# Expert results added onto residual rows in DRAM by the scatter, and a tail worked in halves

## The reference, cut to what matters

```python
x = x + mix
x = x + _hier_moe(_rmsnorm(x, norm_ffn_g), ...)      # 16 experts, each token goes to 2 of one group
y = _rmsnorm(x, norm_final_g)                        # rows of 1024; meta rows are dropped

# in _hier_moe, per token and expert:
act = silu(t @ w_gate_e) * (t @ w_up_e) * comb       # comb is 0 for experts not chosen
out = sum over experts of act @ w_down_e
```

## Time and profile before

| | us |
|---|---|
| median of 3 runs | 772.13 (771.56 to 772.36) |
| the profiled execution, device time | 773.97 |
| its span in the trace | 772.1 |
| PE busy | 751.5 |
| DVE busy | 667.1 |
| ACT busy | 515.4 |
| POOL busy | 97.3 |

### The profile page before, as it was taken

One profiled execution on the slowest core, in us unless ns is written; L12 is line 12 of the kernel. 1 busy time (PEld: TensorE's weight loads), 2 busy tenths in 40 slices (PEclk: granted clock), 3 DMA queues, 4 the chain that ended last, 5 costly groups with the idle time before them and its releaser, 6 DMA issues.

```text
span 772.1 us, 12114 instructions
## 1 busy us (share of the span) xinstructions
PE 751.5 (97%) x4731; PEld 654.5 (85%) x4731; DVE 667.1 (86%) x912; ACT 515.4 (67%) x649; POOL 97.3 (13%) x120
## 2 busy tenths in 40 slices
PE   8999999999999999999999999999999999999994
PEld 4999999877777799999989976888888888888873
DVE  5599999888888878899879686989899989999897
ACT  7433445876868775445695464788888888888863
POOL 0100001223333400000011002011111111110000
PEclk9999999999999999999999999999999999999998
DMA  9935546598899956445449574999999999999972
GB/s 345 362 128 187 190 164 235 184 331 318 299 309 306 364 172 220 164 164 198 168 160 336 219 274 149 336 365 383 379 371 355 386 372 366 354 366 372 351 265 83
DMA packets 39174, 213.28 MB, mean 276 GB/s; under 512 B 7381, under 2 KB 7637, under 8 KB 19244
## 3 DMA queue, kind: packets, MB, share of 16 engines
q1 hardware_dynamic: 23268, 165.39, 58.2%
q0 software_dynamic: 15408, 45.71, 16.8%
q10 hardware_dynamic: 432, 1.31, 0.5%
HBM read 193.45 MB, written 31.65 MB: 292 GB/s over the span
## 4 chain that ended last, share of the span: by engine, by line
PE 67%; DVE 13%; DMA 11%; ACT 4%; issue 3%; POOL 1%; DVEq 0%; ACTq 0%; POOLq 0%
PE bank L1939 34%; PE bank L1663 25%; DMA out_ret_sample<-S_ring 4%; DVE w_lo L1109 3%; DMA out_ret_sample<-xT 3%; DVE conv L1164 3%; DMA out_ret_sample<-S_five 3%; PE bank L1929 2%; DMA xT<-in_state_ret 1%; PE bank L1969 1%; ACT w_hi L764 1%; DMA con<-constants 1%; PE bank L1689 1%; PE bank L1680 1%; PE bank L1721 1%
## 5 line engine op out<-in xcount | busy, mean ns | idle before, releaser
L1663 PE MATMUL bank<-h_hi,w_hi 128*128 128x264 f32 (+1 forms) x640 | 188.6, 295 | 4.2 <-DVE w_lo L1109 3.2
L1663 PE MATMUL bank<-h_hi,w_lo 128*128 128x264 f32 (+1 forms) x640 | 184.9, 289 | 0.0
L1663 PE MATMUL bank<-h_lo,w_hi 128*128 128x264 f32 (+1 forms) x640 | 184.9, 289 | 0.0
L1114 DVE TENSOR_TENSOR ring_lo<-raw,ring_hi 128x2048 fp32r<-128x2048 f32 x72 | 163.6, 2288 | 22.7 <-ACT ring_hi L771 22.6
L1109 DVE TENSOR_TENSOR w_lo<-raw,w_hi 128x1024 fp32r<-128x1024 f32 x112 | 136.6, 1221 | 27.7 <-ACT w_hi L764 27.3
L764 ACT ACTIVATE w_hi<-raw 128x1024 fp32r<-128x1024 f32 x112 | 117.8, 1052 | 52.5 <-PE bank L1663 51.7
L771 ACT ACTIVATE ring_hi<-raw 128x2048 fp32r<-128x2048 f32 x72 | 138.2, 1919 | 19.0 <-PE bank L1939 18.1
L1663 PEld LDWEIGHTS bank<-h_hi,w_hi 128*128 128x128 f32 x640 | 121.3, 190 | 7.7 <-DVE w_lo L1109 4.9
L1663 PEld LDWEIGHTS bank<-h_lo,w_hi 128*128 128x128 f32 x640 | 121.2, 189 | 0.8 <-issue 0.2
L1663 PEld LDWEIGHTS bank<-h_hi,w_lo 128*128 128x128 f32 x640 | 121.0, 189 | 0.0
L1164 DVE SCALAR_TENSOR_TENSOR conv<-u,vec,conv 128x256 f32<-128x256 f32 x240 | 101.8, 479 | 0.6
(11 more groups left out here) (311 smaller groups left out, 1478.1 us busy)
## 6 DMA issues: line engine op xcount, KB each, us to landing
raw<-weights SPq DMA_DIRECT2D x152, 1024.0 KB, 7.2
S_ring<-in_state_ret POOLq DMA_DIRECT2D x20, 512.0 KB, 7.8
out_ret_sample<-S_ring POOLq DMA_DIRECT2D x20, 512.0 KB, 6.5
xT<-in_state_ret POOLq DMA_DIRECT2D x8, 512.0 KB, 6.6
out_ret_sample<-xT POOLq DMA_DIRECT2D x8, 512.0 KB, 7.3
S_five<-in_state_ret POOLq DMA_DIRECT2D x4, 512.0 KB, 5.9
out_ret_sample<-S_five POOLq DMA_DIRECT2D x4, 512.0 KB, 9.7
out_ret_prompt<-S_out POOLq DMA_DIRECT2D x8, 256.0 KB, 7.5
```

What stands on the lines that cost most here:

```text
L1114: dve.tensor_tensor(ring_view(ring_lo, k), raw[raw_slot(NCM + k)][:, :].rearrange("p (k n) -> p k n", k=4), ring_view(ring_hi, k).bitcast( ...
L1663: ins = pe.matmul(out, a[:, k, cols], b[:, k0 + k, :], start=first and k == 0 and j == 0, stop=last and k == ks - 1 and j == 2)
```

## The change

`YD` has one row for each token. After `H2` has landed POOL copies the residual rows `xk` into it (three transfers), in place of clearing it. The scatter of every expert adds in DRAM (`compute_op=ALU.add`), and each scatter waits until the one ahead of it has landed. After the last scatter SP loads `YD` straight into `xk`; no row sums are left on DVE. `idx` and `V_` lose their second set of columns.

The tail works in the order 0, 1, 2 of the tiles. Each of the six last additions lets ACT go on: ACT squares tiles 0 and 1 half by half. The first half's sum goes through an Identity activation (L1105 of the changed kernel) and comes back as the bias of the root.

```diff
             def clear_rows(rd):
...
-            clear_rows(0)
+            pool.wait_ge(zero_ready, 2)
             pool.wait_ge(h2_out, 16 * 3)
+            for tt, (t0, nt) in enumerate(MT):
+                evacuated(pool, ("xk", 0, tt))
+                evacuated(pool, ("xk", 1, tt))
+                pool.dma_start(YD[t0:t0 + nt, :], xk[0:nt, tt, :]).then_inc(rows_out, 16)
...
             def scatter(e, rd):
 
                 evacuated(pool, ("dn", e, 1, rd))
-                pool.indirect_dma_start(YD, bass.IndirectOffsetOnAxis(ap=idx[:, NE + e:NE + e + 1], axis=0), Y[:, e % 2, :], None,
-                                        bounds_check=2 * N - 1, oob_is_err=False).then_inc(y_out[e % 2], 16)
+                if e:
+                    pool.wait_ge(y_out[(e - 1) % 2], scattered(rd) + 16 * ((e - 1) // 2 + 1))
+                elif not rd:
+                    pool.wait_ge(rows_out, 16 * 3)
+                pool.indirect_dma_start(YD, bass.IndirectOffsetOnAxis(ap=idx[:, e:e + 1], axis=0), Y[:, e % 2, :], None,
+                                        bounds_check=N - 1, oob_is_err=False, compute_op=ALU.add).then_inc(y_out[e % 2], 16)
```

```diff
                 for i in range(2):
                     sp.wait_ge(y_out[i], scattered(rd + 1))
-                for n, tt in enumerate((2, 0, 1)):
-                    t0, nt = MT[tt]
-                    sp.wait_ge(chunk_lo, NCE * rd + (YY_CHUNKS[n] + 1 if not rd else NCE))
-                    sp.dma_start(yy[tt][0:nt, :, :], YD[2 * t0:2 * (t0 + nt), :].rearrange("(t c) d -> t c d", c=2)).then_inc(yy_in[tt], 16)
+                for tt, (t0, nt) in enumerate(MT):
+                    if rd:
+                        sp.wait_ge(chunk_lo, NCE * (rd + 1))
+                    sp.dma_start(yy[tt][0:nt, :] if rd else xk[0:nt, tt, :], YD[t0:t0 + nt, :]).then_inc(yy_in[tt], 16)
```

```diff
+            for tt in range(2):
+                square(tt + 1, yy[tt][:, 0:512], xk[:, tt, 0:512], ssq2[:, tt, 0:1])
+                act.wait_ge(fin_ssq, tt + 1)
+                act.activation(ssq[:, tt:tt + 1], ssq2[:, tt, 0:1], ACT.Identity, scale=1.0 / D, bias=eps).then_inc(fin_half, 1)
+            for tt in range(2):
+                square(tt + 4, yy[tt][:, 512:1024], xk[:, tt, 512:1024], ssq2[:, tt, 1:2])
+                act.wait_ge(fin_half, tt + 1)
+                root(tt + 3, tt, ssq2[:, tt, 1:2], ssq[:, tt:tt + 1])
+            square(6, yy[2][0:8, :], xk[0:8, 2, :], ssq2[0:8, 2, 0:1])
+            root(5, 2, ssq2[0:8, 2, 0:1], eps[0:8, :])
...
             y_low(LAST[0], 1)
-            row_sum(0, 2, 1)
-            row_sum(0, 0, 0)
-            row_sum(0, 0, 1)
             y_low(LAST[1], 0)
-            row_sum(0, 1, 0)
             y_low(LAST[1], 1)
-            row_sum(0, 1, 1)
-            dve.wait_ge(sum_done, 3)
+            for tt in range(3):
+                dve.wait_ge(yy_in[tt], 16)
             for k, (tt, j) in enumerate(FINAL):
                 last_added(k + 1, tt, j)
```

More of the change, by code:

```diff
@@ L103, in moe_constants @@
     c[:, 388:404] = np.arange(16, 0, -1)
[L104 to L107, removed]
+    c[:, 404:407] = i[:, None] + 128 * np.arange(3)[None, :] - ABSENT
     return c
@@ L634, in _ @@
             sp.dma_start(gf_b, L["norm_final"]).then_inc(gf_in, 16)
-            for n, tt in enumerate((2, 0, 1)):
-                sp.wait_ge(fin_h, 2 * n + 2)
+            for tt in range(3):
+                sp.wait_ge(fin_h, 2 * tt + 2)
                 if tt == 2:
@@ L1081, in _, with square, root @@
             act.activation(warm[:, 4:5], eps[0:1, :], ACT.Sqrt)
-            for n, tt in enumerate((2, 0, 1)):
+            def square(k, out, src, total):
+                act.wait_ge(fin_y, k)
+                act.activation(out, src, ACT.Square, accum_out=total).then_inc(fin_ssq, 1)
+            def root(n_sq, tt, total, bias):
                 nt = MT[tt][1]
[L1084 to L1088, removed]
+                act.wait_ge(fin_ssq, n_sq)
+                act.activation(rs2[0:nt, tt:tt + 1], total, ACT.Sqrt, scale=1.0 / D, bias=bias).then_inc(fin_std, 1)
+            for tt in range(2):
+                square(tt + 1, yy[tt][:, 0:512], xk[:, tt, 0:512], ssq2[:, tt, 0:1])
+                act.wait_ge(fin_ssq, tt + 1)
+                act.activation(ssq[:, tt:tt + 1], ssq2[:, tt, 0:1], ACT.Identity, scale=1.0 / D, bias=eps).then_inc(fin_half, 1)
+            for tt in range(2):
+                square(tt + 4, yy[tt][:, 512:1024], xk[:, tt, 512:1024], ssq2[:, tt, 1:2])
[3 more added lines that the diff above has]
+            root(5, 2, ssq2[0:8, 2, 0:1], eps[0:8, :])
         @block.vector
@@ L1446, in _ @@
             gained(1, 2)
-            rows = mcon[:, MCON["rows"]:MCON["rows"] + 12].rearrange("p (c v t) -> p c v t", c=2, v=2)
+            rows = mcon[:, MCON["rows"]:MCON["rows"] + 3].rearrange("p (t a) -> p t a", a=1).broadcast_to([128, 3, NE])
             for c in range(2):
-                for v in range(2):
-                    dve.tensor_tensor(V_[:, c, :, v, :], o12[:, c, :, :],
-                                      rows[:, c, v, :].rearrange("p (t a) -> p t a", a=1).broadcast_to([128, 3, NE]), ALU.mult)
+                dve.tensor_tensor(V_[:, c, :, :], o12[:, c, :, :], rows, ALU.mult)
             seen(dve, ("pos",))
@@ L1630, in _ @@
             dve.wait_ge(gf_in, 16)
-            for k, tt in enumerate((2, 0, 1)):
-                scaled(k, tt)
+            for tt in range(3):
+                scaled(tt, tt)
         @block.tensor
@@ L1982, in experts_pe @@
                         evacuated(pe, ("dn", LAST[0], 0, 0))
-                        for tt in (2, 0, 1):
+                        for tt in range(3):
                             opened(("fin", tt, 0))
```

71 lines of the change are left out of this document (33 added, 38 removed).

## The result

The changed kernel takes **777.17 us** (median of 4 runs, 776.46 to 777.98) against 772.25 (771.56 to 772.7) for the kernel before on the same chip: ratio 1.006, 95% interval 1.0048 to 1.0072. It is slower by 4.9 us. The forecast was 772.0, with the range ending at 773.9.

What follows compares the result with a forecast made beforehand. The prediction took PE to set the pace among the experts, with only front and tail mattering. Tail -0.8 and front +0.65 sum to -0.15, applied to the median 772.13 for 772.0 us; range 771.0 to 773.9.

Steps and rivals of the forecast that it cites:

- The experts: Expert stage: adding scatters and smaller `idx` and `V_` cost 0; no wait of PE, pace unchanged.
- the rivals: Alternatives: copies hold back the first gather (slower, 0.13), adding scatter slow (slower, 0.07), tail gives more (faster, 0.05).
- PE sets the pace there: Among the experts PE is busy 20.00 of 20 us, so savings on DVE, ACT or POOL there are worth nothing.
- One expert still 17.68 us: Sign expected in the new profile: each expert takes as long as before, with no wait of PE among the experts.
- the three events: Prediction wrong if PE waits for weights or x_hi mid-experts, scatters wait for `y_out`, or `YD` loads land behind DVE's last x_lo.
- The adding scatters, 0: Experts: each scatter waits for the one before, landed within 8.7 us against 17.68 us between scatters; cost 0.
- The rival of the slow scatter: Experts or tail: adding scatter blocks weight loads (786) or its latency delays the tail (773 to 778); chance 0.07.
- The front, +0.65: Before expert 0: copies ahead of gather 0 delay its data by 0.9 us, less 0.25 PE can spare.
- the rival in which the copies hold the gather back: Front: copies land at about 472, the gather at 473; +1.6 with the tail included, 773.7; chance 0.13.
- The tail, -0.8: After the experts: no row sums, ACT starts 1.26 us earlier, small store last; the span ends 0.8 us earlier.
- the change does nothing that shows: Whole kernel: the two terms are small against PE's 761.9 us, time within 0.2%; the forecast itself, chance 0.75.

## Why the prediction was wrong, step by step

**The experts, +4.2 us: the step that failed.** The prediction said: "The smaller `idx` and `V_` shorten two steps of DVE and six small matmuls that stand behind filler; 0." It counted what the smaller tensors do as operands and not that they move every tensor declared behind them. What the runs showed: with addresses put back and all else changed, the ratio is 0.9997; with the changed addresses in the kernel before, 1.0048. None of the rivals was this mechanism. The statement "PE sets the pace there" was right, and is why 6.6 ns on a matmul came through in full: 1,152 matmuls had no cover. "One expert still 17.68 us" was the sign that failed; the three events that the prediction named for its being wrong (PE waiting in the experts, scatters waiting for `y_out`, late loads of `YD`) did not come. It looked for waits, and a slower PE shows none.

**The adding scatters, 0: right.** Their instruction on POOL takes 2.09 us at the median against 1.54, and they land 8.9 to 11.5 us after issue, 9.7 at the median, where the next one comes 17.98 us later; with addresses as before the experts take 284.31 us. So the new wait of a scatter for the one before it cost nothing, and the loads of the sums (747.6 to 748.4) were in time for the additions at 762.41. The rival of the slow scatter would have looked like this result in its sign, and the cadence of the experts with the addresses put back (17.71) excludes it.

**The front, +0.65: the mechanism right, the size near its upper bound.** Counted from the start of `idx`, the copies were to start at +0.05 and the gather at +1.95. In the changed kernel they started at -0.06 and +1.81, in three of its variants at +0.84 to +1.11 and +2.71 to +2.99, released by the landing of the stores to `H2` in the changed kernel and in two of the variants. Without them the gather starts at +1.20. Their three issues took 1.57 us (forecast 1.6). In the changed kernel the copies landed 3.0 to 4.0 us after issue, the last by 467.8. From its own start to PE's first use the gather then took 4.8 to 5.1 us, in place of 4.3.

Part of the changed kernel's front is the clock, and the two have to be told apart:

```profile
452.00:454.00 2.00, 2.00 (x5) 0.94 (x4) 1.82 (x14) 1.86 (x4) 0.00 (x0) 0.62 1.02 418
454.00:456.00 2.00, 2.00 (x4) 0.76 (x3) 1.90 (x14) 0.36 (x2) 0.00 (x0) 0.53 1.01 258
456.00:460.00 4.00, 4.00 (x17) 2.25 (x16) 2.65 (x11) 2.77 (x5) 0.00 (x0) 1.00 0.92 340
```

These stretches of the changed kernel (columns as in the earlier trace rows) have a granted clock of 0.62 and 0.53, near the lower of its two levels, 1.2 of 2.4 GHz; between 452.5 and 455.9 it is at 0.50. On PE only filler runs there; the 24 router matmuls had ended at 452.0. Of the eleven profiled executions of the whole kernel two fell there and four more at about 468, with code of either kind in both groups, so a fall belongs to an execution and not to the change. The fronts, in us:

| | no fall | fall at 452 | fall at 468 |
|---|---|---|---|
| no copies ahead of gather 0 | 19.2 to 19.3 (4 kernels) | 20.1 | 20.2, 20.3 |
| copies ahead of gather 0 | 20.9 | 21.05 (the changed kernel) | 21.8, 21.9 |

Without a fall the copies cost 1.6 us (20.88 against 19.24), and putting them behind the gathers gives the same 1.6 back. The early fall costs 0.9 where nothing stands ahead of the gather, and only 0.2 with the copies. It makes `idx` 0.8 us late in both cases, but with the copies gather 0 waits for them, and they start with the landing of `H2`, 11.4 to 11.8 us behind the first store of `h` whether the clock fell or not. The forecast had put this start at 10.75 (464.9 - 454.15). So the landing of `H2` was taken 0.7 to 1.0 us too early, and the gather behind the copies lands later than was assumed. 1.6 lies about midway between the forecast's 0.65 and the 2.35 (2.6 - 0.25) of the rival in which the copies hold the gather back.

**The tail, -0.8: the size right, half of the reason not.** Measured -0.58 for the changed kernel and -0.61 to -0.78 for the two with addresses as before and halves. Over all executions profiled, the five old tails take 14.3 to 14.9 us and the six new ones 13.5 to 13.9. From the last `x_hi` on, the first square comes after 3.87 us (5.24 before; forecast 3.98), the first reciprocal after 7.23 (forecast 7.26), and the small store is last. But the half squares did not matter, as the experiments with full squares show, and that the reciprocal came at 7.23 is in part luck. The forecast hung it on the root of a half square. With full squares the root comes 1.3 us earlier (5.25 us behind the last `x_hi`), and the reciprocal comes at 7.18 all the same, held on DVE by what the prediction did not have. What is left of the gain is the row sums taken away and the small tile as the last; no run parted these two.

**Sum.** With the addresses undone the change is worth 0.9997, "the change does nothing that shows", the case that had 0.75. The forecast missed the one part of the change that moves no work, and for the rest it landed on the right sum in part by luck: the profiled executions have the front at +1.6 and the tail at -0.7, together +0.9, and not -0.15. The times of the kernel with addresses put back say -0.2 us (ratio 0.9997), with an interval from -0.8 to +0.5. At least 0.4 us between the parts and the times is not accounted for.

## What to carry to other kernels

When an allocation before a hot loop changes size, compare the start addresses of the loop's operands in both programs, modulo 256 bytes, before anything is timed. For 4-byte matmuls of 512 columns keep what is loaded and what is streamed at equal residues: the price was 3% of each matmul, and no busy share of PE, no wait and no clock in the profile shows it, only the number of instructions in a full stretch and PEld's share. This is not a rule for other shapes: in bfloat16 the distance made no difference, and with 256 columns equal residues were the slowest. And a kernel that is compared for a change of its function should have its addresses held by rooms, or the comparison measures both.

## What the runs showed of the hardware

- 4-byte matmuls of 512 columns, each with its own load of 128: 226.7 ns at a distance of 0 modulo 256 bytes between streamed and loaded operand, 228.9 at 64, and 233 to 234 at 32, 96, 128, 160, 192 and 224. ACT and DVE at work beside them changed this by 1.1 ns at most. With 256 columns it was 120.0 ns at 0 and 113.3 to 118.6 at 32, 64, 128 and 192, and in bfloat16 215.8 at every distance.
- An indirect transfer that adds in DRAM occupied POOL for 2.09 us at the median instead of 1.54 and landed 8.9 to 11.5 us after issue; weight loads in the same kernel landed after 7.3 us against 7.2.
- A gather of 128 rows that was issued behind 1 MB of plain copies on POOL was used 4.8 to 5.1 us after its start, against 4.3 without them.
- The granted clock fell to 0.50 in the front of 6 of 11 profiled executions, and not in the others of like code. Such a front was 0.9 to 1.1 us longer, but only 0.2 us where the slowed work ran beside a longer wait for a transfer.
- Like code reached the end of the mixer at 454.15 in one execution, whose clock was at 0.50 from 247.0 to 250.4, and at 451.3 to 452.0 in ten others. A single profile can be off by more than the effect that is looked for.
